# The combine of a mixture-of-experts layer: as a stage of its own, or inside each step of the experts

## What is computed

```python
g_prob = softmax(t @ w_group_router + b_group_router);  g_w, g_idx = lax.top_k(g_prob, 1)
e_sel = (t @ w_expert_router + b)[group g_idx]                      # 8 experts a group, 4 groups
e_w, e_idx = lax.top_k(softmax(e_sel), 2);  w = g_w * e_w / sum(e_w)   # 2 experts a token
hid = silu(t @ w_gate[e]) * (t @ w_up[e])                           # 1024 -> 256
y = sum over the two experts of w * (hid @ w_down[e])               # 256 -> 1024
x = x + g2 * rms_norm(y, post_norm_ffn)
```

## Time and profile before

| | us |
|---|---|
| median of 3 runs | 975.36 (973.2 to 976.76) |
| the profiled execution's own time | 974.86 |
| its span, first to last instruction | 973.1 |
| PE, DVE, ACT, Pool busy | 940.8, 514.5, 314.2, 220.7 |
| from HBM, to HBM | 178.27 MB, 24.69 MB |

### The profile page before, as it was taken

One profiled execution on the slowest core, in us unless ns is written; L12 is line 12 of the kernel. 1 busy time (PEld: TensorE's weight loads), 2 busy tenths in 40 slices (PEclk: granted clock), 3 DMA queues, 4 the chain that ended last, 5 costly groups with the idle time before them and its releaser, 6 DMA issues.

```text
span 973.1 us, 15261 instructions
## 1 busy us (share of the span) xinstructions
PE 940.8 (97%) x5445; PEld 559.0 (57%) x5445; DVE 514.5 (53%) x939; ACT 314.2 (32%) x644; POOL 220.7 (23%) x270
## 2 busy tenths in 40 slices
PE   7999999999989999998999999989999999999986
PEld 6544444444546666668666665575555555555552
DVE  2266447444765566666578886663333333333337
ACT  3130002222454434442234333243333333333313
POOL 2110001122700570001344422012222222222003
PEclk9999999999999999998999999999999999999999
DMA  9996535000000000006022327978999999999658
GB/s 323 358 332 213 219 116 139 2 1 0 7 0 1 1 1 2 2 1 240 22 88 100 117 84 301 400 252 315 401 416 407 405 406 398 412 416 408 248 211 320
DMA packets 56371, 196.67 MB, mean 202 GB/s; under 512 B 15603, under 2 KB 27003, under 8 KB 40803
## 3 DMA queue, kind: packets, MB, share of 16 engines
q1 hardware_dynamic: 48180, 178.39, 48.3%
q0 software_dynamic: 6816, 17.18, 4.6%
q10 hardware_dynamic: 1296, 0.07, 0.1%
HBM read 178.27 MB, written 24.69 MB: 209 GB/s over the span
## 4 chain that ended last, share of the span: by engine, by line
PE 48%; DVE 3%; DMA 1%; issue 1%; ACT 1%; ACTq 0%; POOL 0%; DVEq 0%; SPq 0%; POOLq 0%
PE PS L1748 16%; PE PS L1597 11%; PE PS L1774 9%; PE PS L1722 2%; PE PS L1559 1%; PE PS L1805 1%; PE PS L1757 1%; DMA y_g<-y_rows 1%; PE PS L1575 1%; PE PS L1609 1%; PE PS L1621 1%; PE PS L1503 1%; DVE y_sum L2414 1%; DVE y_sum L2421 1%; PE PS L1548 1%
## 5 line engine op out<-in xcount | busy, mean ns | idle before, releaser
L1748 PE MATMUL PS<-ring,xg_T 128*64 x736 | 162.7, 379 | 0.8 <-ACT xg_T L1924 0.8
L1748 PE MATMUL PS<-near_gu,xg_T 128*64 128x256 f32 x736 | 162.7, 379 | 0.0
L1748 PEld LDWEIGHTS PS<-ring,xg_T 128*64 128x64 f32 x736 | 100.7, 137 | 60.1 <-issue 13.5
L1597 PE MATMUL PS<-w_out_sb,cat_T 128*128 128x512 f32 x256 | 116.8, 597 | 0.4 <-ACT cat_T L1845 0.4
L1031 PE MATMUL PS<-hT,w_x 128*128 128x512 f32 x256 | 112.1, 594 | 0.0
L1748 PEld LDWEIGHTS PS<-near_gu,xg_T 128*64 128x64 f32 x736 | 100.7, 137 | 0.0
L452 POOL TENSOR_SCALAR rstd<-stat 128x1 f32<-128x1 f32 (+1 forms) x44 | 20.3, 462 | 297.1 <-ACT junk L637 174.5
L1774 PE MATMUL PS<-ring,hid_T 128*64 x184 | 83.8, 598 | 0.5 <-DVE hid_T L2356 0.5
L1774 PE MATMUL PS<-near_dn,hid_T 128*64 128x512 f32 x184 | 83.9, 598 | 0.0
L1031 PEld LDWEIGHTS PS<-hT,w_x 128*128 128x128 f32 x256 | 47.8, 190 | 58.5 <-issue 58.2
L2347 DVE TENSOR_TENSOR hid<-PS,hid_s 128x128 f32<-128x128 f32 x46 | 11.3, 286 | 129.2 <-PE PS L1748 129.1
(11 more groups left out here) (356 smaller groups left out, 1556.3 us busy)
## 6 DMA issues: line engine op xcount, KB each, us to landing
ring<-in_w_gate_dram SPq DMA_DIRECT2D x32, 1024.0 KB
ring<-in_w_up_dram SPq DMA_DIRECT2D x32, 1024.0 KB, 13.8
ring<-in_w_down_dram SPq DMA_DIRECT2D x32, 1024.0 KB, 16.8
ada_later<-in_ada_w_dram SPq DMA_DIRECT2D x16, 1024.0 KB, 4.8
ada_first<-in_ada_w_dram SPq DMA_DIRECT2D x16, 512.0 KB, 9.7
y_g<-y_rows SPq DMA_DIRECT2D x8, 1024.0 KB, 13.1
x_in<-in_x_dram SPq DMA_DIRECT2D x8, 512.0 KB, 7.9
w_out_sb<-in_w_out_dram SPq DMA_DIRECT2D x1, 4096.0 KB, 12.7
```

The lines of the kernel that those rows point to most:

```text
L1597: last = pe.matmul(BANK[sorted(out_banks(t))[j]], cat_T[t % 2][:, k, :], w_out_sb[:, k, j * HALF:(j + 1) * HALF], start=(k == 0), stop=(k ...
L1748: last = pe.matmul(BANK[2 + s_][rows_, 0:FF], xg_T[b][:, k, rows_], gu[u][:, s_, k, :], start=(k == 0), stop=(k == KC - 1))
```

## The change

The stage behind the steps is gone. Each step now finishes the tokens whose *later* row it makes (the row of the expert that comes later in the order of the steps). A token's first row is still scattered to `y_rows`; the rows are weighted when they are copied out of PSUM.

- **The table.** `table` (DVE, once, after `tx(0)`) writes for each of the 2048 entries four numbers: its weight, its place in `y_rows` if it is a first row (else out of bounds), the place of its partner's row if it is a later one, and its token if it is a later one. SP stores them as `ext_rows`; `entries(n)` gathers the 16 bytes of each row of step n into `tab`.
- **A step's end, over three steps.** `scatter(m-1)` stores first rows; `other_rows(m-1)` waits until this scatter has landed, and gathers the partners' rows into `y_o` (zeros, or untouched values, where there is none); `summed` adds `y_e`; `square` (ACT) sums the squares; `root` (Pool, two small operations) makes the inverse root; `residual_rows` gathers rows of `x2_rows` into `x_o`; `finished` (DVE, two operations) scales, adds; `out_rows` scatters to `out`.
- **Buffers.** To make room, `x_g`, `xg_T`, `hid_s`, `hid`, `hid_T` and `x_o` are single (`2 * [...]`). A gather now waits for the transposes of the step before. `y_rows` is zeroed once by an 8 MB DMA early in the kernel.
- **Gone:** y_g, x2_all, w_diag, the sums on PE, SP's stores.

```diff
-        x_g = [place(f"x_g{i}", R_XG + 4096 * i, [P, D]) for i in range(2)]
+        x_g = 2 * [place("x_g", R_XG, [P, D])]
+        y_o = [spent("y_o0", 4096, [P, D]), place("y_o1", R_A + 83968, [P, D])]
+        x_o = place("x_o", R_XG + 4096, [P, D])
+        hid_s = 2 * [spent("hid_s", -2048, [P, FF])]
+        hid = 2 * [spent("hid", -1024, [P, FC, P])]
+        hid_T = 2 * [place("hid_T", R_A + 81920, [P, FC, P])]
...
+            sp.dma_start(y_rows.rearrange("(p a) d -> p a d", p=P), zeros[:, :].unsqueeze(1).to_broadcast([P, 2 * NT, D]))\
+                .then_inc(S["w_up_loaded"], 16)
...
                 def scatter(n):
                     b = n % 2
-                    if n == 0:
-                        pool.wait_ge(S["dst_read"], 1)
+                    counted("tab_here", n + 2)
+                    counted("ye_stored", n)
                     pool.wait_ge(S["ye_act"], n + 1)
                     pool.wait_ge(S["ye_dve"], n + 1)
...
+                def other_rows(n):
+                    counted("ye_stored", n + 1)
+                    counted("ye_stored", n + 2)
+                    counted("other_here", n)
+                    if n >= 2:
+                        pool.wait_ge(S["fin_done"], n - 1)
...
+                def all_out(n):
+                    counted("out_stored", n + 1)
+                    counted("out_stored", n)
...
+                def out_rows(n, x_of):
+                    counted("out_stored", n)
+                    pool.wait_ge(S["fin_done"], n + 1)
...
                 def run(lo, hi):
-                    for n in range(lo, hi):
-                        if n >= 2:
-                            pool.wait_ge(S["tx_done"], n - 1)
-                            gather(pool, n)
-                        if n >= lo + 3:
-                            scatter(n - 3)
-                    for n in range(hi - 3, hi):
-                        scatter(n)
...
+                    for m in range(lo, hi):
+                        if m - 1 >= lo:
+                            scatter(m - 1)
+                        if m - 3 >= lo:
+                            out_rows(m - 3, x_o)
+                        if m - 1 >= lo:
+                            other_rows(m - 1)
+                        if m - 2 >= lo:
+                            root(m - 2)
+                            all_out(m - 2)
+                            residual_rows(m - 2, x_o)
+                        if m + 2 < hi:
+                            pool.wait_ge(S["tx_done"], m + 2)
+                            gather(pool, m + 2)
+                            entries(m + 2)
+                    pool.wait_ge(S["gu_done"], hi)
+                    residual_rows(hi - 2, x_end[0])
+                    residual_rows(hi - 1, x_end[1])
+                    scatter(hi - 1)
+                    other_rows(hi - 1)
+                    out_rows(hi - 3, x_o)
+                    root(hi - 2)
+                    out_rows(hi - 2, x_end[0])
+                    root(hi - 1)
+                    out_rows(hi - 1, x_end[1])
+                    all_out(hi)
...
+                def square(n):
+                    b = n % 2
+                    act.wait_ge(S["fin_sum"], n + 1)
+                    act.wait_ge(S[f"ye_stored{b}"], 16 * (n // 2 + 1))
...
+                def summed(n):
+                    b = n % 2
+                    dve.wait_ge(S[f"other_here{b}"], 16 * (n // 2 + 1))
+                    dve.wait_ge(S["ye_act"], n + 1)
+                    dve.tensor_tensor(y_o[b][:, :], y_o[b][:, :], y_e[b][:, :], ALU.add).then_inc(S["fin_sum"], 1)
+
+                def finished(n, x_of):
+                    y = y_o[n % 2][:, :]
+                    dve.wait_ge(S["fin_root"], n + 1)
+                    dve.scalar_tensor_tensor(y, y, rstd[:, 7, n % NT:n % NT + 1], G2[:, :], ALU.mult, ALU.mult).then_inc(S["fin_step"], 1)
+                    dve.wait_ge(S[f"x_here{n % 2}"], 16 * (n // 2 + 1))
+                    dve.wait_ge(S["fin_step"], n + 1)
+                    dve.tensor_tensor(x_of[:, :], y, x_of[:, :], ALU.add).then_inc(S["fin_done"], 1)
...
                     for n in range(lo, hi):
                         if n + 1 < hi:
                             src = slot_of(dve, 2 * n + 3)
+                        if n - 3 >= lo:
+                            finished(n - 3, x_o)
+                        if n - 2 >= lo:
+                            summed(n - 2)
                         gated(n)
                         th(n)
```

More of the change, by code:

```diff
@@ L243, in hybrid_block @@
         at8 = nc.alloc_sbuf_tensor_at("at8", [P, 8], mybir.dt.uint32, offset=FRONT + 4576)
+        ext = front("ext", 4096, [P, NT, 2, 4])
+        ext_i = ext.bitcast(I32)
+        second = front("second", 4352, [P, 2, NT])
+        spot = front("spot", 4416, [P, 2, NT])
+        SLOTS = 6
+        WEIGHT, FIRST_AT, OTHER_AT, OUT_ROW = range(4)
+        tab = front("tab", 4480, [P, SLOTS, 4])
+        tab_i = tab.bitcast(I32)
+        half_j = front("half_j", 4576, [P, 2, NT])
+        ext_rows = nc.dram_tensor("ext_rows", [2 * T + 1, 4], F32).ap()
+        zeros = place("zeros", R_U + 4096, [P, D])
         R_RT = R_A + 161792
@@ L255, in hybrid_block @@
         he_f, off_f = (late(f"he{i}", 7 + i, [P, 1])[:, :] for i in range(2))
-        base_j, half_j = (late(f"base_j{i}", 9 + i, [P, 2, NT]) for i in range(2))
+        base_j = late("base_j", 9, [P, 2, NT])
         put_f = place("put_f", R_S + 4096 + 128 * 11, [P, NTILE])
@@ L505, in _ @@
             last.then_inc(S["pad_zeroed"], 1)
+            pool.memset(zeros[:, :], 0.0).then_inc(S["masks_made"], 1)
+            pool.wait_ge(S["masks_made"], 2)
             pool.wait_ge(S["kpe_act"], NH2)
@@ L1485, in _ @@
                 steps(pool, run)
-                for t in range(NT):
-                    inverse_root(pool, 7, t, S["ysum_sq"], t + 1)
             @block.tensor
@@ L1795, in _ @@
                 steps(pe, run)
-                pe.wait_ge(S["w_diag"], 1)
-                busy(7, 44)
-                for n, t in enumerate(PE_TILES):
-                    pe.wait_ge(S[f"yg_loaded{t}"], 16)
-                    if n >= 4:
-                        pe.wait_ge(S["o_scaled"], PE_TILES[n - 4] + 1)
-                    for j in range(D // HALF):
-                        for k in range(2):
-                            last = pe.matmul(BANK[n % 4 * 2 + j], w_diag[:, 2 * n + k, :], y_g[t][:, k, j * HALF:(j + 1) * HALF],
-                                             start=(k == 0), stop=(k == 1))
-                    last.then_inc(S["ysum_pe"], 1)
             @block.scalar
@@ L1972, in run @@
                         silu(n)
+                        if n - 2 >= lo:
+                            square(n - 2)
                         if n + 1 < hi:
@@ L1978, in run @@
                             nearer_down(n + 1, *src)
+                    square(hi - 2)
+                    square(hi - 1)
                 steps(act, run)
[L1982 to L1998 removed]
             @block.vector
@@ L2351, in th @@
                     b = n % 2
[L2352 to L2353 removed]
+                    if n:
+                        dve.wait_ge(S["dn_done"], n)
                     for k in range(FC):
@@ L2383, in run @@
                     tx(lo)
+                    if lo == 0:
+                        table()
                     for n in range(lo, hi):
```

180 lines of the change are left out of this document (83 added, 97 removed).

## The result

| | before | after |
|---|---|---|
| median | 974.7 us (973.2 to 976.8, 5 runs) | 1067.7 us (1059.0 to 1071.3, 5 runs) |
| span of the profiled execution | 973.1 | 1056.9 |
| first gather of the steps | 648.1 | 646.7 |
| last down product ends | 930.9 | 1024.6 |
| from there to the end | 42.2 | 32.3 |

The changed kernel takes 1.094 times as long (95% interval 1.091 to 1.097). The forecast of 986.3 us had the direction and not the size: the time is 81 us above it, and 53 above the range. The table says where it went: the tail gave back 9.9 us, and the 23 steps became 95 us longer, 4.1 us each.

The account below looks back on a forecast made before the run. PE was taken to bound the 23 steps, with little DMA room left. 974.9 - 20.6 (Term 1) + 25 (Term 2) + 4 (Term 3) + 0 (Term 4) + 3 (Term 5) = 986.3 us; range 957 to 1015.

Parts of the forecast that it names:

- Term 2: Pool's queue in the steps: landing 5.4 plus 8.0 makes a 13.4 us round against 11.98; +25 us.
- Term 3: DVE and ACT in the steps: residual rows landing late can hold DVE ahead of gated, 0.4 us a step; +4 us.
- Term 5: End of the steps: Pool is behind by about 3 us that the last two steps don't give back; +3 us.
- Term 1: Tail after the last down product: 21.6 us instead of 42.2; -20.6 us.
- Term 4: DMA side in the steps: 8.4 MB extra could make weights late, hidden if steps are 13.4 us long; 0.
- Rival 1: Pool's round: below 11.98 us if landings under load stay under 3.9, so PE keeps its step; 961 us, chance 0.25.
- Rival 2: DVE operations with two SBUF inputs stop Pool's DMA instructions, 1.23 us a round; 1011 us, chance 0.13.

Follow-up runs that it names:

- e1: The changed kernel, with weight loads of experts 6 to 31 cut to an eighth of their bytes: 966.9 us (0.992).
- e2: The kernel before, with Pool waiting for each scatter and every fourth gather to land, then marking it with a memset: 997.1 us (1.022).
- e8: The changed kernel, with each weights DMA split in two (contiguous pieces of 1 and 2 KB instead of 8 KB): 1044.9 us (1.072).
- e4: The changed kernel, with other_rows reading a zeroed tensor nobody writes, so without the wait for the scatter: 1049.7 us (1.076).
- e10: The changed kernel, same work, with Pool's round reordered, finished writing into y_o, and summed and square behind gated, tx and nearer: 1012.5 us (1.038).
- e11: The reordered kernel of e10, with each weights DMA split in two (pieces of 1 and 2 KB): 1012.0 us (1.036).
- e12: The reordered kernel of e10, with weight loads of experts 6 to 31 cut to an eighth of their bytes: 963.1 us (0.987).
- e9: The kernel before, with one x_g instead of two and the gather ahead of the scatter in Pool's queue: 978.7 us (1.002).
- e3: The kernel before, with one x_g instead of two and the gather behind a scatter that waits for y_e: 1125.0 us (1.150).
- e13: The reordered kernel of e10, with residual_rows and out_rows taking only token 0, all other indices out of bounds: 994.1 us (1.020).
- e7: The landing probe e2, with each weights DMA split in two (pieces of 1 and 2 KB): 1000.8 us.

## Why the prediction was wrong

**What bounds the kernel, and the direction: right.** PE's path was full, nothing of the change lies on it directly (e1: 48.00 of 48 us busy with all of it in place), and Pool's round sets the step.

**Term 2, Pool's round: the step that failed, by its first number.** The sum of Pool's own work, 8.0 us, holds row by row. The landing was put at 5.4 us, "near the loaded row", with an upper bound of 6.4. That row was the second gather at 649.64, and the side beside it was not full; I said so and still drew the bound just above it. It measured 9.7 in the median of the changed kernel, and 5.6 to 12.6 in e2. With 9.7 the same formula gives a round of 17.7 and an excess of 111 us in place of 25. The rounds measured 17.4 in the mean under load and 16.5 over all, and the steps became 95 us longer. That the formula comes so near is in part luck, since it has one of two cycles of about the same length; in e8, with a landing of 6.5, it is 1.8 us a round short.
**Terms 3 and 5, the residual and the end.** Term 3 named the right place (the residual's landing holds `finished` ahead of `gated`) and gave it 0.4 us a step. It waited 65.9 us in 15 of the steps, part of it beside Pool's wait. Not seen was the cycle through the single x_o, and this is the second step that failed: removing Pool's wait alone gave back 18 us (e4), and by the sums above the two cycles are nearly equal in length, 17.7 and 17.0 us. Most of both is landings. No run took the second one away alone. Term 5's 3 us have no row of their own; what Pool is behind at the end stands in the 4.7 us of the next part.

**Term 1, the tail: gain over-estimated by 10.7 us.** 32.3 us instead of 21.6 (whose terms add up to 21.4). DVE's last y_e and Pool's rows behind it:

```profile
1024.56 0.75 DVE L2396 TENSOR_SCALAR y_e<-PS,tab 128x512 f32<-128x512 f32 x1 [3.64 <-PE PS L1819]
...
1028.33 1.36 POOL L1483 DMA_INDIRECT x_end<-x_rows,tab  x1 [2.95 <-DMA x_o<-x_rows,tab]
1029.99 1.01 POOL L1466 DMA_INDIRECT y_rows<-y_e,tab  x1 [0.30 <-issue]
...
1046.84 1.07 POOL L1493 DMA_INDIRECT out_dram<-x_end,tab  x1 [3.52 <-DVE x_end L2433]
```

The last scatter starts 4.7 us after y_e is there (0.83 was counted), because three residual gathers stand ahead of it in Pool's queue and the third waits for the first to land. That is 3.9 us. From that scatter to the start of the last out_rows it is 16.85 us, against 16.0 by the prediction's terms. Its landing takes 4.1 us instead of 3.24, and 6.0 more pass from there until the span ends, where 0.6 was counted; what they are the trace doesn't show.

**Term 4, weights: as said, 0.** With long steps they are hidden, and in e10, with steps near 14 us, too. e11 waits for weights, but at the lower rate of its small pieces. What the added bytes cost at steps of 12 us with pieces of 8 KB no run shows.

**Rival 1 (Pool keeps up, 961 us) happened where its condition was made true**: without the load the scatter landed in 3.8 us in e12, below the 3.9 that it asked for, in 4.3, a little above it, in e1, and PE kept its step in both. The times were 966.9 and 963.1 us. Its 961 holds 7 us for the weights' lateness, which these two can't have; without them it is 954, and what lies above is the longer tail.

**Rival 2 (DVE stops Pool) was half right in its mechanism and wrong in its price.** Scatter rows took 1.013 us in the median, but a Pool DMA row that begins while DVE is within such an operation ends 0.9 to 1.0 us after it. DVE's and Pool's timelines at one place:

```profile
891.01 1.28 DVE L2430 SCALAR_TENSOR_TENSOR y_o<-y_o,rstd,G 128x1024 f32<-128x1024 f32 x1 [1.11 <-POOL rstd L457]
```

```profile
891.59 1.72 POOL L1483 DMA_INDIRECT x_o<-x_rows,tab  x1 [0.62 <-issue]
```

891.01 + 1.28 + 1.02 is 893.31, where the Pool row ends. So it lost 0.7 us, not 1.23. From 690 us on nine rows that began within `finished`'s first operation took 1.50 to 2.03 us (2.03 at 729.81, beside DVE's 1.28 from 729.53), together 6 us more than at 1.0 each; most of the others are 1.0 to 1.15. The inference that the prediction took along, that descriptor writing isn't held, does not agree with these rows. Beside landings of 10 us that is small, and e1 has the same operations with PE never stopped. The zeros, the table, the weighted copies and the single hid and xg_T cost nothing that shows in e1.

**The clock** was no term. PE's granted clock fell with the gaps: in the window 792 to 800 us it was 0.65 (0.50, the lower of its two levels, in the first 2.4 us), and a down product that takes 0.59 us at 798.59 took 1.12 after a gap of 9.34 us:

```profile
792.05 1.12 PE L1767 MATMUL PS<-ident,x_g 128*128 128x128 f32 x4 [9.34 <-DMA x_g<-h_rows,idx_i]
...
794.38 1.12 PE L1819 MATMUL PS<-ring,hid_T 128*64 x1
```

From here to the next step's first product at 799.45 it is 5.07 us, where down took 3.62. Pool's scatter behind it started without waiting (803.39, idle 0.30), so it cost nothing in this round. Over all steps it shows. The windows of the steps, before and after (length, busy time of PE, PEld, DVE, ACT, Pool, clock, DMA share, GB/s):

```profile
648.10:930.90 282.80, 280.02 (x2106) 166.35 (x2104) 95.47 (x193) 102.53 (x138) 62.96 (x45) 1.00 0.93 369
```

```profile
646.70:1024.60 377.90, 304.85 (x2105) 173.60 (x2104) 170.07 (x266) 128.25 (x181) 171.04 (x174) 0.91 0.77 283
```

PE is busy 25 us longer with the same products, at a granted clock of 0.91 in place of 1.00; the other 70 of the 95 us are idle time. How much of the 25 us made steps longer no run shows, since the lower clock comes with the gaps; e1, without gaps, has 1.00.

## What to carry to other kernels

Before a DMA that nobody waits for gets a waiter, measure its landing under the load of the stage in which it will be waited for, with a wait and a mark in the old kernel; one that takes 3.3 us unloaded took 7 to 12 here in most cases. Write down every cycle of a pipelined loop with the landings in it (scatter to read back, and buffer filled, used, stored, filled again), and compare each with the step; a buffer made single was nearly free here as long as its transfer still fitted into what is left of the step, and the place in a shared queue decided that (e9, e3). Fusing a stage into a loop whose transfers already fill the DMA engines, as here, trades a tail that is paid once for latency that is paid in each step.

## What the runs showed of the hardware that was not expected

- A scatter of up to 128 rows landed in 3.3 us without load, in 7.1 to 9.4 us alone in its queue beside the weights' queue, and mostly in 10.3 to 11.6 just behind a gather (e2); with six such DMAs a step in flight the medians were 9.2 to 12.5 us (e10).
- A Pool DMA row that begins within a DVE operation of 1024 f32 columns with two SBUF inputs is held and ends 0.9 to 1.0 us after it (rows above), while one that began just before it is not: 1.03 us for the scatter of 803.39, with DVE's sum at 803.46.
- Taking nearly all rows out of such a DMA did not shorten it: 10.6 us against 10.5 (e13). The rows were out of bounds and moved nothing, and the queue's packets stayed 17488. Gathers of 16 bytes a row took 9.0 to 11.0.
- Pieces of weights of 1 and 2 KB instead of 8 KB took the scatter's landing from 10.2 to 7.1 us (e2, e7) and the rate of full engines from 408 to 352 GB/s (before, e11).
- No version tried here with the full work and load beats the kernel before. The best are e11 and e10 at 1012.0 and 1012.5 us. Without load the reordered one is 12 us faster than the kernel before with its load, near to what the shorter tail gave back; the kernel before was not run without load.
